# A ring of weight buffers in an fp32 transformer kernel: low parts in place, and the loops written out

## The reference, cut to what matters

```python
merged = g[:, :, 0] * (ya @ w_branch_a) + g[:, :, 1] * (yb @ w_branch_b) + g[:, :, 2] * (yc @ w_branch_c)
x = x + merged @ w_out
h = rms_norm(x, norm_ffn_g)
u = causal_dwconv(h @ ffn_up, ffn_conv_w, ffn_conv_b)
u_gate, u_val = split(u, 2)
x = x + (gelu(u_gate) * u_val) @ ffn_down
# layers 2 and 3: x = layer_norm(ALPHA * x + mix), silu in place of gelu, layer_norm again after the FFN
```

## Time and profile before

| | us |
|---|---|
| median of 3 runs | 1225.55 (1224.78 to 1227.5) |
| the profiled execution | 1226.56 |
| its span in the profile | 1224.7 |
| PE busy | 1206.6 (99%) |
| VectorE busy | 846.1 (69%) |
| ScalarE busy | 707.7 (58%) |
| GpSimd busy | 406.6 (33%) |
| DMA, share of 16 engines' span | 56.6% |

### The profile page before, as it was taken

How to read it: one execution, slowest core, us unless ns; L and a number is a source line. 1 busy time by engine, 2 the same in 40 slices (tenths; PEclk the granted TensorE clock), 3 DMA queues, 4 the chain that set the end, 5 groups by cost and what they waited for, 6 DMA issues and landing times. The chain is left out here.

```text
span 1224.7 us, 27264 instructions
## 1 busy us (share of the span) xinstructions
PE 1206.6 (99%) x10242; PEld 1183.0 (97%) x10242; DVE 846.1 (69%) x1458; ACT 707.7 (58%) x1228; POOL 406.6 (33%) x376
## 2 busy tenths in 40 slices
PE   8999999999999999999999999999999999999997
PEld 8999999999999999999999999999999999999997
DVE  6868666677777755766677777656766677777655
ACT  5667676445766654566455666644566555666642
POOL 3007304123334302200338343314500348344313
PEclk9999999999999999999999999999999999999998
DMA  7555455664666665555653666664555654666662
GB/s 254 183 168 156 134 153 166 197 182 154 194 187 201 183 191 162 164 164 155 190 185 116 183 190 187 195 190 147 171 157 156 190 187 121 178 199 186 196 189 85
DMA packets 60288, 212.70 MB, mean 174 GB/s; under 512 B 6688, under 2 KB 7968, under 8 KB 60064
## 3 DMA queue, kind: packets, MB, share of 16 engines
q1 hardware_dynamic: 60192, 211.39, 56.6%
HBM read 210.31 MB, written 1.05 MB: 173 GB/s over the span
## 5 line engine op out<-in xcount | busy, mean ns | idle before, releaser
L1393 DVE TENSOR_TENSOR wlo<-raw,whi 128x1024 fp32r<-128x1024 f32 (+1 forms) x400 | 488.5, 1222 | 289.4 <-ACT whi L735 287.5
L1067 PE MATMUL bank<-shifted,whi 128*128 128x256 f32 x2296 | 638.9, 278 | 1.5 <-POOL shifted L669 1.1
L1068 PE MATMUL bank<-shifted,whi 128*128 128x256 f32 x2296 | 636.3, 277 | 0.0
L1069 PE MATMUL bank<-shifted,wlo 128*128 128x256 f32 x2296 | 636.0, 277 | 0.0
L735 ACT ACTIVATE whi<-raw 128x1024 fp32r<-128x1024 f32 (+1 forms) x400 | 415.6, 1040 | 148.0 <-PE bank L1069 134.4
L1067 PEld LDWEIGHTS bank<-shifted,whi 128*128 128x128 f32 x2296 | 431.7, 188 | 3.1 <-POOL shifted L669 1.3
L1069 PEld LDWEIGHTS bank<-shifted,wlo 128*128 128x128 f32 x2296 | 431.7, 188 | 0.0
L1068 PEld LDWEIGHTS bank<-shifted,whi 128*128 128x128 f32 x2296 | 431.1, 188 | 0.0
L636 POOL TENSOR_TENSOR fprod<-ugate,uval 128x256 f32<-128x256 f32 x66 | 99.4, 1506 | 210.1 <-DVE uval L1741 204.5
L1067 PE MATMUL bank<-fhi,whi 128*128 128x256 f32 x528 | 146.8, 278 | 0.0
L1069 PE MATMUL bank<-fhi,wlo 128*128 128x256 f32 x528 | 146.5, 277 | 0.0
(11 more groups left out here) (212 smaller groups left out, 1283.3 us busy)
## 6 DMA issues: line engine op xcount, KB each, us to landing
raw<-in_w_win SPq DMA_DIRECT2D x140, 512.0 KB, 3.6
raw<-in_w_up SPq DMA_DIRECT2D x132, 512.0 KB, 3.6
raw<-in_w_down SPq DMA_DIRECT2D x48, 448.0 KB, 3.8
raw<-in_w_merge SPq DMA_DIRECT2D x32, 512.0 KB, 4.1
raw<-in_w_out SPq DMA_DIRECT2D x24, 512.0 KB, 3.8
raw<-in_w_down SPq DMA_DIRECT2D x24, 512.0 KB, 3.6
x<-in_x SPq DMA_DIRECT2D x4, 256.0 KB, 3.9
rgw<-in_rg_w SPq DMA_DIRECT2D x1, 1024.0 KB, 10.2
```

The lines of the kernel that those rows point to most:

```text
L1067: pe.matmul(ps, whi[:, slot, w], hi, start=first, stop=False)
L1068: pe.matmul(ps, whi[:, slot, w], lo, start=False, stop=False)
L1069: return pe.matmul(ps, wlo[:, slot, w], hi, start=False, stop=last)
L1393: dve.tensor_tensor(wlo[:, n % RING, w], raw[:, n % RING, w], whi[:, n % RING, w].bitcast(f32), ALU.subtract) \
```

## The change

The low part is written over the arrived weights: `wlo` gets the same memory as `raw`, in five slots, and `whi` gets four. A slot of `raw` is then free only when PE is done with the unit, so the load of unit n waits for PE's end of n-5, and the high part of n for PE's end of n-4. ACT and VectorE make their parts one unit further ahead (`n + 3` for `n + 2`, `n + 4` for `n + 3` in the `win` stages), and one more of each before the first unit. `repeat` writes all rounds out. With that a temporary of the squares in the down stages can use four buffers throughout.

```diff
-RING = 3
+RAW_RING, HI_RING = 5, 4
...
-        raw = sb("raw", [P, RING, 8 * P])
-        whi = sb("whi", [P, RING, 8 * P], r32)
-        wlo = sb("wlo", [P, RING, 8 * P], r32)
+        whi = sb("whi", [P, HI_RING, 8 * P], r32)
+        with ExitStack() as landing:
+            raw = sb("raw", [P, RAW_RING, 8 * P], stack=landing)
+        wlo = sb("wlo", [P, RAW_RING, 8 * P], r32)
+
+        def raw_of(n, blocks):
+
+            return raw[:, n % RAW_RING, 0:blocks * P]
...
-            rounds = count // per
-            lo, hi = (1 if peel_first else 0), rounds - 1
-            n0 = START[name]
-            for i in range(lo * per):
-                body(n0 + i, i, 0)
-            if hi > lo:
-                with eng.Fori(lo, hi) as it:
-                    for i in range(per):
-                        body(n0 + i, i, it)
-            for i in range(hi * per, count):
-                body(n0 + i, i, 0)
+            for i in range(count):
+                body(START[name] + i, i, 0)
...
-                wait(sp, split_lo, n - RING + 1, it, per)
+                wait(sp, unit_done, n - RAW_RING + 1, it, per)
...
-            for n in range(1, RING):
+            for n in range(1, HI_RING - 1):
                 load(n)
             sp.dma_start(const[:, P:], args["const"][:, P:]).then_inc(load_const, 16)
             sp.dma_start(ipos[:], args["positions"]).then_inc(load_pos, 16)
+            load(HI_RING - 1)
             sp.dma_start(rgw[:], args["rg_w"]).then_inc(load_rg, 16)
             sp.dma_start(poolw[:], args["pool_w"]).then_inc(load_rg, 16)
-            for n in range(RING, WIN1 + MERGE1):
+            for n in range(HI_RING, WIN1 + MERGE1):
...
-                wait(act, arrived[n % RING], 16 * (n // RING + 1), it, 16 * per // RING)
-                wait(act, unit_done, n - RING + 1, it, per)
-                act.activation(whi[:, n % RING, 0:blocks * P], raw[:, n % RING, 0:blocks * P], ACT.Copy).then_inc(split_hi, 1)
+                wait(act, arrived[n % RAW_RING], 16 * (n // RAW_RING + 1))
+                wait(act, unit_done, n - HI_RING + 1, it, per)
+                act.activation(whi[:, n % HI_RING, 0:blocks * P], raw_of(n, blocks), ACT.Copy).then_inc(split_hi, 1)
...
             hi_part(2)
+            hi_part(3)
...
                 if n < last:
-                    hi_part(n + 3)
+                    hi_part(n + 4)
...
                     if i or not isinstance(it, int):
-                        hi_part(n + 2, it, 6)
+                        hi_part(n + 3, it, 6)
...
-                dve.tensor_tensor(wlo[:, n % RING, w], raw[:, n % RING, w], whi[:, n % RING, w].bitcast(f32), ALU.subtract) \
+                dve.tensor_tensor(wlo[:, n % RAW_RING, w], raw_of(n, blocks), whi[:, n % HI_RING, w].bitcast(f32), ALU.subtract) \
...
                     if t >= begun:
-                        lo_part(START[name] + t + 2)
+                        lo_part(START[name] + t + 3)
```

More of the change, by code:

```diff
@@ L306, in build @@
         load_x = [sem(f"load_x{i}") for i in range(KT // 2)]
-        arrived = [sem(f"arrived{i}") for i in range(RING)]
+        arrived = [sem(f"arrived{i}") for i in range(RAW_RING)]
         split_hi, split_lo = sem("split_hi"), sem("split_lo")
@@ L516, in load @@
                 array, t, first, blocks = UNITS[n]
-                wait(sp, split_lo, n - RING + 1, it, per)
+                wait(sp, unit_done, n - RAW_RING + 1, it, per)
                 tiles = per // len(DOWN_PARTS) if array.startswith("w_down") else per
                 src = args[array][t:t + 1] if isinstance(it, int) else args[array][bass.ds(it * tiles + t, 1)]
-                sp.dma_start(raw[:, n % RING, 0:blocks * P], src[:, :, first * P:(first + blocks) * P].rearrange(
-                    "o p n -> (o p) n")).then_inc(arrived[n % RING], 16)
+                sp.dma_start(raw_of(n, blocks), src[:, :, first * P:(first + blocks) * P].rearrange(
+                    "o p n -> (o p) n")).then_inc(arrived[n % RAW_RING], 16)
             def loads(name, count, per):
@@ L687, in layer_norm @@
                     pool.wait_ge(dev_squared, KT * i + t + 1)
-                    ring = 2 if which[:3] == "ln2" and t < 4 else 4
-                    add_tile(t, 0, tmp[:, t % ring, :], tmp[:, 0, :], added_q, ACCQ[which])
+                    add_tile(t, 0, tmp[:, t % 4, :], tmp[:, 0, :], added_q, ACCQ[which])
                 pool.wait_ge(mean_copied, i + 1)
@@ L936, in merge @@
                         for u in range(per_tile):
-                            hi_part(first + per_tile * t + u + 2)
+                            hi_part(first + per_tile * t + u + 3)
                     t -= 1
@@ L963, in wout @@
                     if t >= begun:
-                        hi_part(first + t + 2)
+                        hi_part(first + t + 3)
                     if t == 0:
@@ L1023, in _ @@
             norm_root("ffn", RMS_EPS)
-            hi_part(START["up1"] + 2)
+            hi_part(START["up1"] + 3)
             norm_hi("ffn", dev)
@@ L1028, in _ @@
             norm_root("final", RMS_EPS)
-            hi_part(START["win20"] + 2)
+            hi_part(START["win20"] + 3)
             norm_hi("final", x)
@@ L1051, in _ @@
                 norm_root(f"ln1{l}", LN_EPS)
-                hi_part(START[f"up2{l}"] + 2)
+                hi_part(START[f"up2{l}"] + 3)
                 norm_shift(f"ln1{l}", False)
@@ L1063, in _, with product_of @@
         def _(pe):
-            def product_of(ps, slot, block, hi, lo, first, last):
+            def product_of(ps, n, block, hi, lo, first, last):
                 w = slice(block * P, (block + 1) * P)
-                pe.matmul(ps, whi[:, slot, w], hi, start=first, stop=False)
-                pe.matmul(ps, whi[:, slot, w], lo, start=False, stop=False)
-                return pe.matmul(ps, wlo[:, slot, w], hi, start=False, stop=last)
+                pe.matmul(ps, whi[:, n % HI_RING, w], hi, start=first, stop=False)
+                pe.matmul(ps, whi[:, n % HI_RING, w], lo, start=False, stop=False)
+                return pe.matmul(ps, wlo[:, n % RAW_RING, w], hi, start=False, stop=last)
             def begin(n, result, it=0, per=0, rper=0, banks=3):
@@ L1478, in _ @@
             lo_part(2)
+            lo_part(3)
             neg, z, z2, poly = (soft[:, i, :] for i in range(4))
@@ L1675, in steps @@
                 if n < last:
-                    lo_part(n + 3)
+                    lo_part(n + 4)
                 for name, *a in SLOTS.get(n, []):
@@ L1732, in body @@
                 def body(n, i, it):
-                    lo_part(n + 2, it, 6)
+                    lo_part(n + 3, it, 6)
                     q = KT + UPT * f + i
@@ L1787, in _ @@
             for l in range(LAYERS2):
-                lo_part(START[f"win2{l}"] + 2)
+                lo_part(START[f"win2{l}"] + 3)
                 waiting, base = None, KT * (1 + l)
```

23 lines of the change are left out of this document (12 added, 11 removed).

## The result

The changed kernel takes 1232.82 us (median of 4 runs, 1231.85 to 1235.19), beside 1225.82 us for the kernel before on the same chip: ratio 1.0058 (95% interval 1.0046 to 1.0070). It is slower by 7 us, where 1222.4 was forecast. Its profiled execution took 1232.17 us with a span of 1229.8, which is 5.6 and 5.1 us more than before.

A forecast was written before the change was run, and what follows sets the result against it. PE, busy in 99% of the span, was taken as the bound. 1226.56 - 8.4 gained + 5.5 lost gave 1223.7 us, 1222.7 against the median, 1222.4 with 0.3 for the first up stage; range 1216.9 to 1228.5.

The forecast's parts named there:

- Part 1: Loops written out: gain of 0 to 1.8 us, 1.8 taken, from the first down stage.
- its ring: ACT, VectorE and GpSimd cycle per tile in up stages: falls from 5.52 to 5.30 us, below PE's 5.48.
- long spacing: First down stage: 0.354 us per set of three products against 0.34 elsewhere; 1.8 us expected to go.
- Part 2: Parts made one unit further ahead: 4.7 us gained in later up stages, 1.5 and 0.4 at down-stage starts.
- rivals C and D: C: longer spacing in other down stages, 1226.0 us, chance 0.16. D: written-out cycle stays at 5.48 or more, 1229.4, 0.07.
- credited to the lead at the start of the later down stages: PE's wait for the last product's low part gone, 0.5 us each; the following unit's lateness, 0.2 each.
- Part 3: Later weight loads delay low parts and VectorE's work behind them at three kinds of stage end: 5.5 us lost.
- in the middle of a stage nobody needs the delayed work soon: Deviation and residual behind late low parts cost nothing mid-stage, as banks give a unit or more.
- the size after the output projections: VectorE's residual 0.6 us late after each of three output projections, 1.8 us in all.
- The two other places: Residual 1.3 us late after two down stages, 2.6 us; gating 0.55 late before two output projections, 1.1 us.
- Rival B: Landing becomes the last wait, at ACT's copy with VectorE behind; landings of 4.6 us give 1229.4 us; chance 0.14.
- Part 4: VectorE writes the low part over its input: nothing, or 0.02 us a unit; nothing taken.

The follow-up runs named there:

- six-slot kernel with late loads: Changed kernel with six arrival slots, but every load still waiting for PE to be done with the unit five back: 1231.37 us, 1.0043.
- all three repairs: Changed kernel with rotation and scores before the low part, output-projection parts behind the tile's own work, 10 fillers before the norm's sums: 1227.20 us, 1.0013.

## Why the prediction was wrong

**Part 1 was right, and its ring too.** The 1.8 us of long spacing in the first down stage went with the loops alone, in full. That the body was only 1.13 us shorter there is another term: PE's wait for the last product grew by 0.7. The two other down stages gained 0.8 each and two up stages 1.2, 3.4 us over the whole by the ratio, without any change in the lead. On the Trainium skill's rule of taken branches ("Runtime: NRT & Kernel Launch", "Instruction fetch mechanics") the gain would have been larger; the run shows 0.28% for all loops together, which does not tell a fetch from the register work.

**Part 2 was right in its sum.** The up bodies fell by 5.4 us and the down bodies by 3.6, 9.0 together, where Parts 1 and 2 had 8.4 and the sum 0.3 more for the first up stage. The ring ran at 5.30 us as forecast; rivals C and D did not come. What was credited to the lead at the start of the later down stages (0.5 and 0.2 us each) the loops alone bring. In the first down stage the wait for the last product became 0.2 us shorter, not 0.5.

**Part 3 failed, in two steps.** The first is the sentence that in the middle of a stage nobody needs the delayed work soon. It took units to be 2.74 us apart. In a ramp two of them end together after a pause of 11 us, so the sixth and seventh load leave late and as a pair, and the rotation for PE stands behind their low parts. The rotation is in none of the prediction's terms. That cost 5.5 us in the two `win` bodies, which one exchange in VectorE's list gave back. For the same reason the output projection's first late pair (landed at 639.0 and 641.5) was not worked off at its end: ACT and VectorE did not catch up in the 23 us of the stage.

The second is the size after the output projections: 0.6 us each was worked out from the landing alone, as if VectorE came to the arrival without a backlog. The landing was even quicker (3.16 us for the last one). But the last low part began 1.2 us after its high part was there: the one before it had taken 1.80 us behind GpSimd's addition, and a deviation and a residual stood between the two. It then took 1.77 us itself, again behind an addition. ACT's square, VectorE's deviation and the parts wait for each other in program order. The residual came 1.94 us later than before in layer 2 and 1.04 in layer 3; GpSimd's sums made 2.6 and 1.7 of it, and the way from them to the first unit, with the clock low for 6.8 us, the remaining 1.2 and 1.8. Together 3.8 and 3.5. These are the profiled execution's; in the six-slot kernel with late loads, with like waits and 3.4 us of low clock, the remainder was 0.3 and 0. In layer 1, which has no deviation there, the forecast loss of 0.6 did not come at all (-0.1).

The two other places were overrated: 0.7 us for 1.3 after each down stage, and nothing for 0.55 before each output projection.

Rival B had the right side and the right place (ACT's copy waits for the landing, VectorE stands behind it), but 1229.4 us, 3.4 below the time, came from landings of 4.6 us. They fell to 3.3. Lateness came from when loads were issued. Part 4 was not tried by itself; the kernel with the old leads, which also works in place, is level with the one that has only the loops, so it costs nothing that can be seen.

## What to carry to other kernels

- A deeper lead and a later load are one bargain: count the time from the event that frees the slot to the first instruction that stands behind the arrival on any engine. Count it where units end in pairs or after a pause, not at the steady pace.
- Work that is ahead of need belongs behind work that somebody waits for in an engine's list. Here one such exchange was worth 6.0 us (1.0058 to 1.0012). It did not make the five-slot kernel with the deeper lead faster than the kernel before, nor did all three repairs.
- Lead is worth having only in stages that lack it. With five slots and the loops written out, the old leads stand at 0.9972 of the kernel before, the deeper lead in `up` alone at 0.9954, and everywhere at 1.0058.

## What the runs showed of the hardware

- In the norm ahead of `up` in layers 2 and 3 the granted clock fell in 15 of 18 norms with the same fillers. At 3.4 us of low clock the norm took up to 0.7 us longer, at 6.8 us 1.2 to 2.0. The same waits of PE (3.1 and 2.2 us) were followed by 6.8 us in one kernel and by 3.4 in another. In the norm ahead of `up1`, with nearly the same rows ahead, a window's clock was 0.62 in one execution and 1.00 in another, which is worth 1.3 us.
- The 132 loads of 512 KB for `up` land in 3.3 us at the median; the second of two that are issued 0.37 us apart is later: after 3.5 to 4.2 and 4.4 to 5.6 us in the eight pairs of the changed kernel.
- A VectorE subtract of 1024 columns (1.23 us alone) and a GpSimd addition of 256 (0.72) that overlap: the first to begin keeps its time (1.22 us at the median of 61 subtracts), the later one waits. Beginning 0.02 us behind an addition the subtract took 1.80 us; an addition that began inside a subtract took up to 1.73 and ended 0.60 us after it.
